# A hybrid decoder step: other load order, chunk schedule and GpSimd order around the output projection

## The reference, cut to what matters

```python
z = h @ w_in + b_in                                  # eight sections of 1024
o_a, s_new = hgrn2_branch(...)                       # gated recurrence
o_b, buf_new = conformer_conv_branch(...)            # depthwise convolution, layer norm, silu
merged = concatenate([sigmoid(gate_a) * o_a, sigmoid(gate_b) * o_b], -1) @ w_out
x = x + g1 * merged
h2 = rmsnorm(x, norm_ffn_w) * (1.0 + sc2) + sh2
gg, uu = split(h2 @ w_ffn_in, 2, -1)
x = x + g2 * ((silu(gg) * uu) @ w_ffn_out)
y = rmsnorm(x, norm_final_w)
```

## Time and profile before

| | us |
|---|---|
| median of 3 runs | 2036.57 (2036.46 to 2040.33) |
| the profiled execution's own time | 2040.33 |
| its span, first to last instruction | 2038.6 |
| PE busy, share of the span | 1964.9, 96% |
| DVE, ACT, POOL busy | 1310.1, 666.8, 246.2 |
| mean granted TensorE clock | 0.987 of full |

### The profile page before, as it was taken

How to read it: one execution, slowest core, us unless ns; L and a number is a source line. 1 busy time by engine, 2 the same in 40 slices (tenths; PEclk the granted TensorE clock), 3 DMA queues, 4 the chain that set the end, 5 groups by cost and what they waited for, 6 DMA issues and landing times.

```text
span 2038.6 us, 39363 instructions
## 1 busy us (share of the span) xinstructions
PE 1964.9 (96%) x15960; PEld 1883.4 (92%) x15960; DVE 1310.1 (64%) x1792; ACT 666.8 (33%) x1070; POOL 246.2 (12%) x245
## 2 busy tenths in 40 slices
PE   6699999999999999999989989999999999999997
PEld 3599999999999999998989989999999999999997
DVE  2776978787887879787676655554445544455544
ACT  2421222313131313132574423333343333433332
POOL 0430010101010001002132384600000000000000
PEclk9799999999999999999989999999999999999998
DMA  7422222223222222222267644444444544445443
GB/s 256 161 76 56 75 77 75 77 65 88 63 71 81 68 75 60 81 65 82 96 199 231 188 120 128 141 134 140 134 138 137 153 138 133 139 141 150 138 134 93
DMA packets 408485, 237.32 MB, mean 116 GB/s; under 512 B 16167, under 2 KB 402887, under 8 KB 408320
## 3 DMA queue, kind: packets, MB, share of 16 engines
q1 hardware_dynamic: 408336, 235.20, 39.0%
HBM read 211.91 MB, written 24.11 MB: 116 GB/s over the span
## 4 chain that ended last, share of the span: by engine, by line
PE 84%; DVE 7%; ACT 2%; POOL 2%; DMA 2%; issue 1%; SPq 0%; DVEq 0%; ACTq 0%; POOLq 0%
PE Z L811 74%; PE R L836 2%; PE R L892 1%; PE R L758 1%; DMA ada_w<-in_w_ada_dram 1%; PE R L842 1%; DVE w_lo L1186 1%; DVE ta L1351 1%; PE R L918 1%; ACT w_hi L1667 1%; PE R L925 1%; DMA mbuf<-merged_scratch 1%; DVE k L1215 1%; PE R L927 1%; DVE x L1555 1%
## 5 line engine op out<-in xcount | busy, mean ns | idle before, releaser
L811 PE MATMUL Z<-h_hi,w_hi 128*128 128x352 f32 x2592 | 695.7, 333 | 18.4 <-POOL h_lo L1956 15.6
L811 PE MATMUL Z<-h_hi,w_lo 128*128 128x352 f32 x2592 | 671.9, 323 | 0.0
L811 PE MATMUL Z<-h_lo,w_hi 128*128 128x352 f32 x2592 | 671.1, 323 | 0.0
L1667 ACT ACTIVATE w_hi<-w_raw 128x1024 fp32r<-128x1024 f32 (+1 forms) x316 | 329.5, 1043 | 944.3 <-PE Z L811 924.7
L1186 DVE TENSOR_TENSOR w_lo<-w_raw,w_hi 128x1024 fp32r<-128x1024 f32 (+1 forms) x306 | 379.0, 1238 | 383.5 <-ACT w_hi L1667 375.1
L811 PEld LDWEIGHTS Z<-h_hi,w_hi 128*128 128x128 f32 x2592 | 451.8, 189 | 38.1 <-issue 26.4
L811 PEld LDWEIGHTS Z<-h_hi,w_lo 128*128 128x128 f32 x2592 | 463.0, 189 | 0.0
L811 PEld LDWEIGHTS Z<-h_lo,w_hi 128*128 128x128 f32 x2592 | 461.4, 189 | 0.0
L1334 DVE SCALAR_TENSOR_TENSOR yb<-up,vec,yb 128x1024 f32 (+1 forms) x240 | 308.3, 1285 | 29.8 <-DVE yb L1334 3.7
L811 PE MATMUL Z<-act_hi,w_hi 128*128 128x352 f32 x528 | 170.2, 322 | 0.0
L811 PE MATMUL Z<-act_hi,w_lo 128*128 128x352 f32 x528 | 169.5, 321 | 0.0
(11 more groups left out here) (284 smaller groups left out, 2050.1 us busy)
## 6 DMA issues: line engine op xcount, KB each, us to landing
w_raw<-in_w_ffn_in_dram SPq DMA_DIRECT2D x132, 512.0 KB, 3.8
w_raw<-in_w_in_dram SPq DMA_DIRECT2D x64, 512.0 KB, 5.1
w_raw<-in_w_out_dram SPq DMA_DIRECT2D x48, 512.0 KB, 4.0
w_raw<-in_w_ffn_out_dram SPq DMA_DIRECT2D x48, 512.0 KB, 3.8
aw<-in_w_ada_dram SPq DMA_DIRECT2D x32, 512.0 KB, 4.2
w_raw<-in_w_ffn_out_dram SPq DMA_DIRECT2D x24, 384.0 KB, 3.4
ada_w<-in_w_ada_dram SPq DMA_DIRECT2D x8, 1024.0 KB, 7.7
mbuf<-merged_scratch SPq DMA_DIRECT2D x32, 176.0 KB, 4.1
```

Of the source, the lines that this page charges most:

```text
L811: last = mm(out, w[:, kt, :], x(kt, g), start=first and kt == 0 and m == 0, stop=last_block and kt == n - 1 and m == 2)
L1667: A(w_hi[b.par][:, 0:n, :], w_raw[b.par][:, 0:n, :], ACT.Copy).then_inc(w_hi_ready, 1)
```

## The change

Three parts. The table `M_AT` moves the splitting of chunks 16 to 31 one tile earlier (beside tiles 0 to 5 instead of 1 to 6), and puts chunks 40 to 47 four each beside tiles 14 and 15, instead of two each beside tiles 12 to 15. On SP the loads are reordered. POOL does the gated chunks of group 2 behind the `h2` passes of group 0 instead of ahead of them.

```diff
-M_AT = {1: range(16, 19), 2: range(19, 22), 3: range(22, 25), 4: range(25, 28), 5: range(28, 30), 6: range(30, 32),
-        **{n: range(2 * n + 16, 2 * n + 18) for n in range(8, 16)}}
-RESIDUAL_AT = {0: (1,), 4: (2,), 5: (3,), 10: (4,), 11: (5,)}
+M_AT = {0: range(16, 19), 1: range(19, 22), 2: range(22, 25), 3: range(25, 28), 4: range(28, 30), 5: range(30, 32),
+        8: range(32, 34), 9: range(34, 36), 10: range(36, 38), 11: range(38, 40), 14: range(40, 44),
+        15: range(44, 48)}
@@ sync engine
+            load_residual(0)
             load_out(2)
-            load_residual(0)
+            load_residual(1)
             load_out(3)
             store_gate(7)
-            load_out(4)
             for i in range(2):
                 sp.wait_ge(gb_stored[i], 16 * NJ // 2)
             ahead = iter(range(M2, G * M2))
-            for c in range(3):
+            for c in range(MBUF):
                 load_m(next(ahead))
             for n in range(G * NJ):
                 if n < G * NJ - 2:
-                    if n:
-                        load_out(2 * n + 4)
+                    load_out(2 * n + 4)
                     load_out(2 * n + 5)
-                for part in RESIDUAL_AT.get(n, ()):
+                if n in (1, 3):
                     sp.wait_ge(m_split, M2)
-                    load_residual(part)
-                if n < 4:
-                    load_m(next(ahead))
+                    load_residual(n + 1)
+                    load_residual(n + 2)
                 for _ in M_AT.get(n, ()):
@@ gpsimd engine
                 root(g)
-                if g == 0:
-                    gated_group(2)
                 pool.wait_ge(*evac(Idx(R_X2 + 2 * g + 1)))
                 ...
+                if g == 0:
+                    gated_group(2)
```

## The result

| | before | after |
|---|---|---|
| median, us | 2037.17 (4 runs) | 2049.34 (2047.14 to 2051.76, 4 runs) |
| the profiled execution, us | 2040.33 | 2049.11 |
| its span, us | 2038.6 | 2047.4 |
| mean granted clock | 0.987 | 0.985 |

The ratio is 1.0056, with a 95% interval of 1.0044 to 1.0068: the changed kernel is slower by 9 to 14 us. The page of after, against the earlier trace rows: busy times have hardly moved, as should be where no work was added.

The account below looks back on a forecast made before the run. PE, 96% busy, was taken to bound the kernel, so only its gaps or clock count. Terms 2.7 + 6.0 - 0.6 + 1.8 - 2.3 + 4.5 - 2.8 - 0.8 + 1.7 gave +10.2 us: 2046.8 us, range 2037 to 2054.

Parts of the forecast that it names:

- old waits: PE's earlier small waits, 0.38 us and some 0.2 beside, go since gated chunk 24 is early: -0.6 us.
- Step 1: Chunks 16 to 18 beside tile 0: ACT rounds them first, so block 3 is late: +2.7 us.
- Step 2: Residual pairs behind tiles 1 and 3: blocks 8 and 12 late by 3.0 us each, +6.0; old waits -0.6.
- rival of absorbed pairs: DMA takes the residual pairs without PE noticing: +2.5 us, 2039.1 us; chance 0.20.
- worse than summed: Pairs cost 4.1 us each and two more gaps lose the clock at 1.7 each: 2052.4 us; chance 0.16.
- Step 3: POOL's earlier h2 slows DVE at tiles 10 and 11, +1.8 us; tiles 13 to 15 stop paying, -2.3.
- Step 4: Four chunks beside tiles 14 and 15: gap of 3.4 us at block 31, 1.1 at block 33, +4.5 together.
- "faster" rival: POOL's eight passes shrink below 30 us, no gap at block 31, pairs absorbed: 2031.6 us; chance 0.08.
- Step 5: Fills: root(1) finds POOL idle, -2.8 us; square sum wait stays in part, -0.8.
- the last rival: Fill gap stays because DVE's mean is late: +2.8 us, 2049.6 us; chance counted within the forecast's 0.56.
- Step 6: New gaps at blocks 3, 8, 12 and 31 bring one drop to 1.2 GHz: +1.7 us (0 to 6.5).

Follow-up runs that it names:

- kernel 7: Changed kernel with residual pieces spread as before, POOL's gated chunks in pairs between h2 passes, chunks 16 to 18 rounded and split behind block 3: 2038.9 us, ratio 0.9998.
- kernel 8: Kernel 7 with block 4 loaded ahead of the seven chunks: 2036.0 us, ratio 0.9984 against the kernel before.
- kernel 2: Kernel before plus the POOL part alone, chunks 40 to 47 four each beside tiles 14 and 15, loads as before: 2039.0 us, ratio 1.0003.
- kernel 5: Kernel before, but POOL makes group 2's gated chunks in pairs behind h2 passes 1 to 4 of group 0: 2032.4 us, ratio 0.9970.
- kernel 9: Kernel before with residual pieces 2 and 3 loaded behind tile 1, 4 and 5 behind tile 3: 2047.3 us, ratio 1.0039.
- kernel 4: Changed kernel with the start's loads and chunks 16 to 31 as before, pairs and POOL part kept: 2048.2 us, ratio 1.0044 against the kernel before.
- kernel 3: Changed kernel with residual pieces 2 to 5 one each behind tiles 4, 5, 10, 11 as before: 2042.9 us, ratio 1.0019 against the kernel before.
- kernel 1: Changed kernel with its POOL part undone, chunks 40 to 47 two each beside tiles 12 to 15: 2046.4 us, ratio 1.0051 against the kernel before.
- kernel 6: Kernel before with residual pieces 2 to 5 one each behind tiles 1 to 4; profiled twice, the first at a low clock: 2042.9 us, ratio 1.0019.

## Why the prediction was right, step by step

The forecast was +10.2 us, and measured were +12.2 by the medians of that session (interval 9 to 14) and +10.2 in the trace, counted from block 2 (8.8 between the two spans, and the 1.4 of before's start). The sum hit, its terms less so:

| step | forecast | measured | where |
|---|---|---|---|
| 1, chunks beside tile 0 | +2.7 | +3.3 | block 3 |
| 2, pairs | +6.0 | +5.1 | blocks 8, 9, 12 |
| 2, old waits | -0.6 | -0.7 | blocks 10, 11, 16 |
| 3, tiles 10 and 11 | +1.8 | +0.7 | blocks 20 to 27 |
| 3, tiles 13 to 15 | -2.3 | -2.3 | blocks 28 to 33 |
| 4, four chunks in a row | +4.5 | +4.5 | block 31 alone |
| 5, `root(1)` | -2.8 | -3.0 | block 36 |
| 5, square sums | -0.8 | -1.9 | block 34 |
| 6, the clock | +1.7 | +4.6 | blocks 4, 13, 32 |

**Step 1** went as worked out: ACT takes the three chunks as they land, then block 3 at 1063.10 (forecast: near 1063), and PE waits. The price is 3.3 and not 2.7 because PE wanted block 3 at 1062.3 already (1065.45 - 3.17; forecast 1063.1), after a shorter 1.2 GHz stretch.

```profile
1061.00 0.99 ACT L1823 ACTIVATE m_hi_a<-mbuf 128x352 fp32r<-128x352 f32 x2 [5.44 <-DMA mbuf<-merged_scratch]
1062.69 0.50 ACT L1823 ACTIVATE m_hi_a<-mbuf 128x352 fp32r<-128x352 f32 x1 [0.70 <-DMA mbuf<-merged_scratch]
1063.10 1.04 ACT L1665 ACTIVATE w_hi<-w_raw 128x1024 fp32r<-128x1024 f32 x1
```

Kernels 7 and 8 moved ACT's order and one load, and neither mended it; the prediction had the cause as "can't go earlier", which stands.

**Step 2** had the right sign, nearly the total, and a wrong split. The old waits (-0.7) can't be credited to it: 0.5 of them is block 16's, and that wait is missing in kernels 2, 5 and 9 as well, where nothing was done about it. Block 8 paid 0.9, block 9 1.1 and block 12 2.9 us, not 3.0 each at 8 and 12. The loads of blocks 8 and 12 landed 7.5 and 7.7 us after their issue, where "8 or more" was forecast and 5.9 was the worst in the earlier trace rows:

```profile
L460 SPq DMA_DIRECT2D w_raw<-in_w_out_dram x1: 379/379/379, 1077.4 to 1077.4; - x1
DMA to landing us min/median/max: 7.5/7.5/7.5
...
L460 SPq DMA_DIRECT2D w_raw<-in_w_out_dram x1: 438/438/438, 1097.1 to 1097.1; - x1
DMA to landing us min/median/max: 7.7/7.7/7.7
```

The model was block 16 of before: asked for 8.0 us before PE wanted it (1113.82 - 1105.82), landed after 5.9, late by 0.4; with 3.0 more to land it came to 3.4. Both loads took about 1.3 us less to land than that sum has. Block 8 was also asked for 9.1 us ahead (1086.48 - 1077.40), and came 0.9 late; block 12 only 7.2 us ahead (1104.30 - 1097.06), and came 2.9 late. So the 3.0 is right for block 12 because two errors nearly cancel, and wrong for block 8. The prediction's reason for taking 3.0 instead of 3.4, that PE's gap of step 1 gives DMA some room, no kernel here tests: where that gap is absent and the pairs stay (kernels 4 and 9), the chunks of tile 2 are loaded behind the pair as well, and block 7 waits for them. That the head start of seven chunks keeps the first pair from block 7, the prediction didn't see; it is why the change's parts don't add. The rival of absorbed pairs is refuted by kernels 3 and 9 (7.6 us less without the pairs; interval 1.0027 to 1.0052 with them alone). Of the rival "worse than summed" the clock half came (two more drops), the 4.1 us a pair did not.

**Step 3** was mis-sized for tiles 10 and 11. POOL's first pass begins at 1144.58 us, as forecast (1134.5, and 10.0 by which the fill itself is later in this trace). DVE splits the chunks of tile 10 at 1149.07 and those of tile 11 at 1156.74, so both tiles have POOL beside them. Over 1144 to 1160 us a chunk took DVE 959 ns, near the 1028 of the earlier trace rows, but `w_lo` 1423 ns in the mean against 1935, and PE waited 0.16 us once:

```profile
L1184 DVE TENSOR_TENSOR w_lo<-w_raw,w_hi 128x1024 fp32r<-128x1024 f32 x5 | 7.1, 1423 | 5.2 <-ACT w_hi L1665 5.2
L1432 DVE TENSOR_TENSOR m_lo_a<-mbuf,m_hi_a 128x352 fp32r<-128x352 f32 x4 | 3.7, 959 | 0.0
```

The 2.3 us of tiles 13 to 15 came out to the decimal, but not all of what was measured is the step's. It includes block 28's wait (0.42), which the forecast had left out. That came of a weight load, which ACT found late while POOL had not yet begun its passes:

```profile
1160.08 1.06 ACT L1667 ACTIVATE w_hi<-w_raw 128x1024 fp32r<-128x1024 f32 x1 [1.92 <-DMA w_raw<-in_w_out_dram]
```

No other trace here has that wait, nor the 0.2 to 0.4 us that blocks 29 and 30 of before took more, so 0.9 of the 2.3 us was not the change's to save. And kernel 5 has POOL's passes and two chunks a tile together at tiles 12 to 15: there `w_lo` takes 1529 ns over 1145 to 1175 us and blocks 28 to 33 lose 1.1 us, not 2.3. The Trainium skill, page "SBUF — State Buffer", section "Who interferes with whom", has the loser of that contention blocked fully; the rows show 1423 to 1935 ns against 1247, so how much it costs differs from place to place (I take it, by which POOL instructions lie beside, which no kernel tested), and PE pays only what exceeds the slack.

**Step 4** held in sum. POOL ended the passes at 1181.1 us (forecast 1170.2 + 10.0 = 1180.2; they took 36.6 us, where the "faster" rival needed less than 30), ACT waited for the first gated chunk until 1182.08, and rounded block 31 behind the fourth:

```profile
1181.10 8.44 POOL L2051 TENSOR_TENSOR mbuf<-mbuf,yb 128x352 f32<-128x352 f32 x7
```

```profile
1182.08 0.50 ACT L1823 ACTIVATE m_hi_b<-mbuf 128x352 fp32r<-128x352 f32 x1 [4.28 <-POOL mbuf L2051]
...
1185.36 0.50 ACT L1823 ACTIVATE m_hi_b<-mbuf 128x352 fp32r<-128x352 f32 x1 [0.67 <-POOL mbuf L2051]
1185.76 1.04 ACT L1665 ACTIVATE w_hi<-w_raw 128x1024 fp32r<-128x1024 f32 x1
```

The gap was 4.5 us instead of 3.4 because PE was ready for block 31 earlier: at 1184.26 (1188.79 - 4.53), which is 1174.3 in the frame of before, where step 3's 1.8 us had put it at 1175.4. What step 3 had too much, step 4 had too little. Block 33 had no gap instead of 1.1: the longer gap and the slow clock behind it left chunk 47 the time to arrive (argued, not tested). Kernel 2 shows the same gap without the loads' edits, kernel 5 its absence.

**Step 5**: `root(1)` found POOL idle and PE waits for it no more, against the last rival. The square sums gained 1.9 us instead of 0.8. In kernels 5, 7 and 8, which have no gap at block 31, they gained 1.1; in after and kernels 2, 3 and 4, which have it, 1.9. So 0.8 of it goes with that gap; that this is because PE then comes to the sums later, and DVE no later, is argued.

**Step 6** failed as a number. One drop was forecast; each of the three gaps of 2.9 us or more was followed by one, 1.3 to 1.7 us apiece. The reasoning that a late next load would hide the drop at blocks 8 and 12 did not hold at block 12 (block 13 came 1.7 us later again). That the sum was still right is luck: 2.9 us too little here and 0.6 in step 1, against 0.9, 1.1 and 1.3 too high in steps 2, 3 and 5. In this trace the rule of the Trainium skill, page "TensorE: Matmul & The Clock Gate", part 1 (the slow clock is the default, and activity releases it), was nearer than my count: every new long gap was paid twice. Kernel 9's 2.17 us at block 12 were not.

## What to carry to other kernels

Where an engine works in order, a table that moves small work "earlier" puts it ahead of whatever stands next; ask when its data lands, not when it is wanted. A long block of one job in front of a shared engine's other job is better cut into pairs ahead of their due times (kernel 5) than swapped whole (the change). Price a new PE gap of about 3 us with some 1.7 us more for the clock (1.2 to 2.9 us here). Don't add the prices of two edits on one queue: how far ahead the small loads are asked for (three chunks or seven) decided which work a burst made late, and how much it cost.

## What the runs showed of the chip that was not expected

The clock behind a gap is not settled by the gap's length. Behind 2.79 us in the trace of before it stayed at 2.4 GHz; behind the same wait of 2.78 us in kernel 1 it fell to 1.2 GHz for about 3.4 us. Kernel 9 had 2.17 us at block 12 without a stretch, kernel 8 had 2.10 us at block 4 with one of 3.4 us. Behind the 2.0 us for the square sums it stayed in before and kernel 1, and fell in kernels 6 (second profile) and 9. Stretches were 3.4 us long, or 6.8 us (one each in before and kernels 2, 7 and 9, two in kernel 4). What decides between them is open.

```profile
1210.66 0.88 PE L849 MATMUL R<-ident,rs 128*128 128x128 f32 x6 [2.78 <-POOL rs L2086]
```

```profile
1211.70:1215.10 3.40, 3.40 (x15) 3.40 (x14) 1.18 (x2) 1.06 (x1) 0.00 (x0) 0.57 0.00 0
```

The medians differ by 12.2 us, the stage by 10.2, or by 11.6 if the time that before's trace alone lost at blocks 16 and 28 to 30 (1.4 us) is counted as its bad luck too. The interval of the ratio (9 to 14 us) holds all three, and what is left is not settled.
